# Third stage of a hybrid decoder trunk run in two passes over its tiles, with the next weights split inside them

## The chip, the cores and the metric

The kernel runs on one core of a Trainium2 chip. A core has TensorE for matmuls (PE in the profile, PEld for its weight loads), VectorE (DVE), ScalarE (ACT) and GpSimd (POOL), and SyncE (SP), which here only issues DMAs. The metric is the device time of one execution in microseconds (us), lower is better.

## The reference

The trunk has two layers over 16 meta tokens and 2048 tokens of width 1024, in float32. What the change touches is the end of layer 0, the shared keys and values, and the input and output of layer 1:

```python
        h = h + gated_deltanet_mixer(h, ...)          # ends with  o @ w_out
    kv = rmsnorm(h, kv_norm) @ kv_w + kv_b            # k gets the rotary embedding
    proj = rmsnorm(h, norm_g) @ w_in                  # queries and gate z of layer 1
    q = apply_rope(proj[..., :SWA_Q_W] + b_q)
    o = sink_attention(q, k, v, ...) * jax.nn.silu(z)
    h = h + o @ w_out
    y = rmsnorm(h, final_norm)                        # meta tokens dropped
```

Each matmul with weights is done as three, of a high and a low part of either operand (high x high, high x low, low x high). Weights are split for that into a high part (ACT: a copy that rounds, with the norm's gain as scale) and a low part (DVE: the rest), chunk by chunk, from a staging buffer that a DMA fills.

## The kernel before

Four stages run one after the other, each with its own buffers and semaphores: normalise_and_transpose, gated_deltanet, output_and_shared_kv (the third stage, about 1674 to 2216 us of the trace) and attention (the fourth). Within a stage every engine has its own program, in order, and waits on semaphores.

The third stage works on 17 tiles of 128 tokens, T = 0 the meta tokens. For tile T it loads o (load_o, line 1436), splits it on ACT (split_o, line 1499) and POOL (line 1662), multiplies by w_out (out_projection, line 1684: two halves b of 24 matmuls into ps_h[b]), adds the residual on DVE (add_residual, line 1580, into h1), normalises on ACT (normalise, line 1506), transposes on TensorE (transpose, line 1715), splits the transposed tile into hT (high_part on ACT, low_part on DVE), and multiplies hT by w_kvz (kv_gate, line 1694: 24 matmuls for keys and values, 48 for the gate). DVE and ACT then make keys (keys_values, line 1598) and gate (gate_part, line 1618, with gate_sigmoid on ACT), SP stores h1, hT, v, kT and gate.

The order within the tile loop (tiles, line 1403) is in step: out_projection(T), kv_gate(T - 1), transpose(T) on TensorE (line 1725). So while the chain from the residual of tile T to its hT runs, TensorE has the 72 matmuls of the tile before. SP's step (line 1445) issues the loads of x and o of tile T + 1 first. hT[0] and hT[1], o_s, o_raw and each ps bank are single buffers; h1 and the rotary table cs have two.

Ahead of the loop all weights are split: 8 chunks of w_out (512 KB) and 16 of w_kvz (256 and 512 KB in turn), over three staging buffers (hn, gate and h1's second half, lines 1397 to 1400; loads at line 1480, ACT at 1565, DVE at 1650 and 1652). The meta tile's first product runs along with them, everything after it waits for all 24.

The fourth stage takes hT of 16 tiles from memory. It starts by splitting 8 chunks of w_q (lines 1935, 2040, 2176), with the first query projection following chunk by chunk (line 2286); then 8 chunks of w_out_b between its first two steps (run, line 1842: `between` after step(-1)), and only after them does SP go on to hT of tile 1. Before that SP issues 22 small and middle loads for the keys and values of the meta tokens and of tile 0. step(t) on TensorE (line 2353) mixes the logits and values of tile t with the output projection of tile t - 1 and the query projections of t + 1 and t + 2; its second full one is step(1).

Of the kernel before, what the change touches and what calls it, by code (L numbers as in the profile page):

```python
# [8 lines left out]
P = 128  # L9
# [1318 lines left out]
def output_and_shared_kv(nc, x, meta, w_out, w_kvz, gains, kv_b, rope, consts, oT_d, oTm_d, h1_d, hT_d, gate_d, kT_d, v_d):  # L1328


    with nc.cleanup_on_exit(), ExitStack() as ctx:
# [11 lines left out]
        kv = sb("p3_kv", [P, KVW])  # L1343
        swapped = sb("p3_swapped", [P, KVW // 2])
        kv_bias = sb("p3_kvb", [P, KVW])
        kT = sb("p3_kT", [P, 2, P])
        gate = sb("p3_gate", [P, 2, FB])
        sig = sb("p3_sig", [P, FB])
        cs = sb("p3_cs", [P, 2, 2 * HD])
# [10 lines left out]
        const_in = sem("p3_const_in")  # L1360
        w_in = [sem(f"p3_w_in{n}") for n in range(3)]
        w_hi = sem("p3_w_hi")
# [12 lines left out]
        hT_lo = sem("p3_hT_lo")  # L1375
        kv_ps = sem("p3_kv_ps")
# [9 lines left out]
        hT_out = sem("p3_hT_out")  # L1386
# [5 lines left out]
        N_CONST = 3  # L1392
        block = ctx.enter_context(nc.Block())

        stage = (hn[:], gate[:].rearrange("p b k -> p (b k)"), h1[:, 1, :])
        chunks = [(wo, kc, slice(0, D), w_out, None) for kc in range(KC)]
        for kc in range(KC):
            chunks += [(wk, kc, slice(0, KVW), w_kvz, kc), (wk, kc, slice(KVW, KZ), w_kvz, KC + kc)]  # L1400


        def tiles(eng, step):

            step(0, 0, True, False)
            step(1, 1, True, True)
            step(2, 0, True, True)
            with eng.Fori(1, NT // 2 - 1) as j:
                for s in (1, 0):
                    step(2 * j + (2 - s), s, True, True)  # L1410
            step(NT - 1, 1, True, True)
            step(NT, 0, True, True)
            step(NT + 1, 1, False, True)

        def is_meta(T):
            return isinstance(T, int) and T == 0

        def rows_of(T):
            return META if is_meta(T) else P

        @block.sync
        def _(sp):
            def load_x(T, s):
                if isinstance(T, int) and T == 2:
                    sp.wait_ge(hn_ready, 1)
                elif not (isinstance(T, int) and T < 2):
                    sp.wait_ge(h1_out[s], 16 * ((T - 1) // 2))
# [1094 lines left out]
```

## Time and profile before

| | before |
|---|---|
| median of 3 runs | 2982.18 us (2980.31 to 2986.79) |
| the profiled execution's own time | 2984.5 us |
| its span, first to last instruction | 2982.5 us |
| mean granted TensorE clock | 0.938 |
| busy PE / DVE / ACT / POOL | 86% / 53% / 38% / 20% of the span |
| third stage | about 1674 to 2216 us |
| fourth stage | about 2217 us to the end |

The busy shares are means over stages with different limits, so they are to be read stretch by stretch. The granted clock is the share of full speed that the chip gave TensorE: 1.00 is 2.4 GHz, 0.50 is 1.2 GHz, and a value between is a stretch that had both. In a timeline each row is a run of equal instructions on one engine; in brackets stands how long the engine was idle before it, and what released it. PE, PEld, DVE, ACT and POOL are the engines, SPq is SP's queue of DMA issues.

### The profile page before, as it was taken

Reading aid. Unit: us, or ns where it says so; the run is one execution under the profiler, and the core shown is the slowest. Engines: PE = TensorE matmul, PEld = TensorE weight load, DVE = VectorE, ACT = ScalarE, POOL = GpSimd, SP = SyncE. Lnnn points to the kernel's source line nnn. Section 1 sums busy time; section 2 is a strip of 40 time slices with the busy share of each in tenths; the row PEclk is TensorE's granted clock in tenths of the full one; section 3 lists DMA queues with packets and bytes.
Section 4 is the critical chain, followed back from the end, with each engine's and each line's share of the span. In section 5 each row is a group of like instructions: output and inputs, shape, how many; then the busy total and the mean of one; then the engine's idle time right before and its main releaser. Section 6 shows DMA issues by size and latency. Waiting matters only on the chain. (4 is left out here: it accounts for less than half of the span.)

```text
span 2982.5 us, 51249 instructions
## 1 busy us (share of the span) xinstructions
PE 2575.0 (86%) x17497; PEld 2284.2 (77%) x17497; DVE 1586.5 (53%) x3692; ACT 1122.8 (38%) x3278; POOL 595.6 (20%) x509
## 2 busy tenths in 40 slices
PE   5468888899999999999998569999966999999996
PEld 4367777888888888888887348888855778778875
DVE  4256666676777677777676322222224444444443
ACT  4244454544444444444443323333323232323222
POOL 0043333311111121111111000000002232322321
PEclk8689999999999999999998579999987999999998
DMA  9764354534436443443441334333333121121211
GB/s 249 226 238 149 116 179 138 172 125 138 129 110 208 123 132 122 136 132 114 144 129 45 115 115 138 108 128 130 106 133 129 64 80 57 62 79 64 70 49 45
DMA packets 272982, 367.27 MB, mean 123 GB/s; under 512 B 74626, under 2 KB 191442, under 8 KB 272882
## 3 DMA queue, kind: packets, MB, share of 16 engines
q1 hardware_dynamic: 231762, 340.64, 35.0%
q10 hardware_dynamic: 41120, 25.37, 2.9%
q8 instruction: 54, 0.88, 0.1%
q14 instruction: 46, 0.38, 0.0%
HBM read 246.96 MB, written 118.98 MB: 123 GB/s over the span
## 5 line engine op out<-in xcount | busy, mean ns | idle before, releaser
L1176 PE MATMUL p_psp<-xg,p_whi 128*128 128x264 f32 x4096 | 847.5, 297 | 25.6 <-POOL p_wlo L1107 19.6
L1176 PEld LDWEIGHTS p_psp<-xg,p_whi 128*128 128x128 f32 x4096 | 666.7, 194 | 28.7 <-issue 26.4
L1176 PE MATMUL p_psp<-xg,p_wlo 128*128 128x264 f32 x2048 | 614.6, 300 | 0.0
L1176 PEld LDWEIGHTS p_psp<-xg,p_wlo 128*128 128x128 f32 x2048 | 397.9, 194 | 0.0
L2235 PE MATMUL p_psq<-p_wq,p_hT 128*128 128x512 f32 x768 | 216.0, 419 | 39.2 <-DVE p_wq L2176 28.7
L954 DVE SCALAR_TENSOR_TENSOR p_acc<-p_proj,p_taps,p_acc 128x528 f32<-128x528 f32 x288 | 242.3, 841 | 8.2
L1680 PE MATMUL p_psh<-p_wo,p_o 128*128 128x512 f32 (+1 forms) x816 | 198.4, 403 | 27.1 <-DVE p_wo L1650 23.3
L975 DVE TENSOR_TENSOR p_prod<-p_Xb,p_blk 32x4 f32<-32x4 f32 (+13 forms) x448 | 202.2, 451 | 5.6
L1680 PEld LDWEIGHTS p_psh<-p_wo,p_o 128*128 128x128 f32 (+1 forms) x816 | 149.9, 186 | 69.3 <-issue 20.6
L2235 PEld LDWEIGHTS p_psq<-p_wq,p_hT 128*128 128x128 f32 x768 | 139.9, 195 | 73.9 <-issue 22.6
L2235 PE MATMUL p_pso<-p_wo,p_oT 128*128 128x512 f32 x768 | 189.2, 399 | 5.1 <-DVE p_oT L2130 5.1
L836 ACT ACTIVATE p_sig<-p_sig 128x528 f32<-128x528 f32 x128 | 82.6, 645 | 278.6 <-DVE p_sig L956 278.2
L1680 PE MATMUL p_psz<-p_wk,p_hT 128*128 128x512 f32 x768 | 176.7, 389 | 0.0
L2235 PEld LDWEIGHTS p_pso<-p_wo,p_oT 128*128 128x128 f32 x768 | 142.2, 190 | 37.0 <-DVE p_oT L2130 8.8
L1680 PEld LDWEIGHTS p_psz<-p_wk,p_hT 128*128 128x128 f32 x768 | 144.2, 188 | 29.9
L1107 POOL TENSOR_TENSOR p_wlo<-p_wraw,p_whi 128x512 fp32r<-128x512 f32 x72 | 100.2, 1402 | 257.4 <-ACT p_whi L817 256.8
L1662 POOL TENSOR_TENSOR p_o<-p_oraw,p_o 128x1024 fp32r<-128x1024 f32 (+1 forms) x17 | 38.8, 2281 | 489.4 <-ACT p_o L1504 489.4
L1983 ACT ACTIVATE p_logits<-p_logits,p_top 128x144 f32<-128x144 f32 x256 | 102.6, 402 | 79.9 <-DVE p_top L2091 79.9
L2339 PEld LDWEIGHTS p_psq<-p_v,p_pT 128*128 128x128 f32 x992 | 119.2, 192 | 16.5 <-issue 11.4
L828 ACT ACTIVATE p_proj<-p_psp 128x264 f32<-128x264 f32 x256 | 99.8, 390 | 72.8 <-PE p_psp L1176 70.7
L1999 ACT ACTIVATE p_out<-p_h 128x1024 f32<-128x1024 f32 x16 | 16.9, 1058 | 278.7 <-DVE p_h L2138 278.7
L2339 PE MATMUL p_psq<-p_v,p_pT 128*128 128x64 f32 x992 | 117.5, 271 | 0.0
(265 smaller groups left out, 4746.3 us busy)
## 6 DMA issues: line engine op xcount, KB each, us to landing
p_whi<-w_dram SPq DMA_DIRECT2D x92, 512.0 KB, 4.3
p_wlo<-w_dram SPq DMA_DIRECT2D x92, 512.0 KB, 5.4
p_wraw<-w_a_in SPq DMA_DIRECT2D x36, 512.0 KB, 6.1
w_dram<-p_whi SPq DMA_DIRECT2D x34, 512.0 KB, 4.1
w_dram<-p_wlo SPq DMA_DIRECT2D x34, 512.0 KB, 5.2
xg<-xT_dram SPq DMA_DIRECT2D x8, 2112.0 KB, 13.1
hT_dram<-p_hT SPq DMA_DIRECT2D x32, 512.0 KB, 2.9
p_hT<-hT_dram SPq DMA_DIRECT2D x32, 512.0 KB, 4.3
```

The lines of the kernel that those rows point to most:

```text
L828: nc.scalar.activation(proj[:, f % 2, 3 + half_ * HALF:3 + (half_ + 1) * HALF], ps_p[half_][:, 0:HALF], ACT.Copy).then_inc(proj_read, 1)
L836: ins = nc.scalar.activation(v, v, ACT.Exp, scale=-1.0)
L954: nc.vector.scalar_tensor_tensor(a, p[:, part:part + GW], w, a, ALU.mult, ALU.add).then_inc(tap_done, 1)
L975: link(nc.vector.tensor_tensor(t3, x3[:, 0:i, 0:i].rearrange("p j c -> p c j"), b3[:, 0:i, i].unsqueeze(1).to_broadcast([rows, i, i]), ALU ...
L1107: nc.gpsimd.tensor_tensor(w_lo[:, f, cols], w_raw[:, f % 2, cols], w_hi[:, f, cols].bitcast(f32), ALU.subtract).then_inc(lo_ready, 1)
L1176: ins = nc.tensor.matmul(ps_p[half_][:, 0:HALF], (w_hi, w_lo)[i][:, f, kc * P:(kc + 1) * P], xg[:, g % 2, j, kc, half_ * HALF:(half_ + 1) ...
L1662: nc.gpsimd.tensor_tensor(o_s[1][:, :, 0:rows], o_raw[:, :, 0:rows], o_s[0][:, :, 0:rows].bitcast(f32), ALU.subtract).then_inc(o_lo, 1)
L1680: last = nc.tensor.matmul(out, stationary[i][:, kc, 0:rows], moving(j, kc), start=kc == 0 and n == 0, stop=kc == KC - 1 and n == 2)
L1983: last_ = nc.scalar.activation(logits[:, s_, :], logits[:, s_, :], ACT.Exp, bias=top[:, s_:s_ + 1], accum_out=den[:, s_:s_ + 1])
L1999: link(nc.scalar.activation(out[:], h[:], ACT.Square, accum_out=rinv[:]))
L2235: ins = nc.tensor.matmul(banks[b][:], stationary[i][:, kc, :], weights[j][:, kc, b * FB:(b + 1) * FB], start=kc == 0 and n == 0, stop=kc = ...
L2339: last_ = nc.tensor.matmul(ps_q[b][:, cols], pT[:, g % 2, x, n * P:(n + 1) * P], v[:, slot, kvh * HD:(kvh + 1) * HD], start=False, stop=g ...
```

## The change

The third stage goes over its tiles twice. The first pass does, per tile, the output projection, the residual, the normalising, the transposes and the split of hT, which is stored for all 17 tiles (the meta tile's in a new array hTm). The second loads hT again, two buffers ahead (in the buffers that held o), and does keys, values and gate. Only w_out is split ahead of the first pass. Each tile T = 0 to 15 of the first pass also loads and splits one chunk of w_kvz; each tile T = 1 to 8 of the second one chunk of w_q, into the buffers that w_out had, which now outlive the stage (first_w) and are handed to attention. o is split into two buffers by turns; o_raw, kv, swapped, sig and kT share one buffer (work), and kv_bias and cs lie in h1's second half. All loops of the stage are written out instead of a hardware loop. The product's halves are taken apart: the transposes of the tile before stand between them, and the turning of the keys stands between the two halves of the gate. The fourth stage has no w_q, no gain, and splits w_out_b in two lots of four chunks, after step(-1) and after step(0), over two staging buffers; SP's load of hT of tile 1 comes ahead of the first lot, h1 of tile 0 behind the second.

The diff, cut to its core:

```diff
--- before.py
+++ after.py
-        wo = [sb(f"p3_wo{n}", [P, KC, D], f32r) for n in range(2)]
+        T_ALL = NT + 1
+        wo = wq = first_w
         wk = [sb(f"p3_wk{n}", [P, KC, KZ], f32r) for n in range(2)]
-        o_raw = sb("p3_oraw", [P, KC, P])
-        o_s = [sb(f"p3_o{n}", [P, KC, P], f32r) for n in range(2)]
+        o_s = [[sb(f"p3_o{s}{n}", [P, KC, P], f32r) for n in range(2)] for s in range(2)]
+        hT_in_sb = o_s
...
-        stage = (hn[:], gate[:].rearrange("p b k -> p (b k)"), h1[:, 1, :])
-        chunks = [(wo, kc, slice(0, D), w_out, None) for kc in range(KC)]
-        for kc in range(KC):
-            chunks += [(wk, kc, slice(0, KVW), w_kvz, kc), (wk, kc, slice(KVW, KZ), w_kvz, KC + kc)]
-
-
-        def tiles(eng, step):
-
-            step(0, 0, True, False)
-            step(1, 1, True, True)
-            step(2, 0, True, True)
-            with eng.Fori(1, NT // 2 - 1) as j:
-                for s in (1, 0):
-                    step(2 * j + (2 - s), s, True, True)
-            step(NT - 1, 1, True, True)
-            step(NT, 0, True, True)
-            step(NT + 1, 1, False, True)
-
-        def is_meta(T):
-            return isinstance(T, int) and T == 0
-
-        def rows_of(T):
-            return META if is_meta(T) else P
+        early = (hn[:], gate[:].rearrange("p b k -> p (b k)"), h1[:, 1, :])
+        k_stage = gate[:].rearrange("p b k -> p (b k)")
+        q_stage = hn[:]
...
+        K_CHUNKS = [(kc, cols, g) for kc in range(KC) for cols, g in ((slice(0, KVW), kc), (slice(KVW, KZ), KC + kc))]
+
+        def k_chunk_of(T):
+
+            return T if T < 2 * KC else None
+
+        def q_chunk_of(T):
+            return T - 1 if 1 <= T <= KC else None
...
+            def load_x(T):
+                s = T % 2
+                if T == 1:
+                    sp.wait_ge(w_lo, KC)
+                elif T >= 2:
+                    if T >= 3:
+                        sp.wait_ge(h1_out[s], 16 * ((T - 1) // 2))
+                    sp.wait_ge(hn_ready, T - 1)
...
+            def load_k_chunk(n):
+                sp.wait_ge(w_lo, KC + n)
+                kc, cols, _ = K_CHUNKS[n]
+                sp.dma_start(k_stage[:, 0:cols.stop - cols.start], w_kvz[:, kc, cols]).then_inc(k_in, 16)
+
+            def load_q_chunk(kc):
+                sp.wait_ge(w_lo, 3 * KC + kc)
+                if kc == 0:
+                    sp.wait_ge(hT_ps, T_ALL)
+                    sp.wait_ge(h_ps, 2 * T_ALL)
+                sp.dma_start(q_stage, w_q[:, kc, :]).then_inc(q_in, 16)
...
+            def load_hT(T):
+
+                s = T % 2
+                sp.wait_ge(h_ps, 2 * T_ALL)
+                sp.wait_ge(hT_out, 32 * (T + 1))
+                if T >= 2:
+                    sp.wait_ge(kv_ps, T - 1)
+                if T >= 3:
+                    sp.wait_ge(z_ps, 2 * (T - 2))
+                for part in range(2):
+                    sp.dma_start(hT_in_sb[s][part][:, :, 0:rows_of(T)].bitcast(f32), hT_home(T, part)
+                                 ).then_inc(hT_in[s], 16)
...
+            for T in range(T_ALL + 1):
+                if T + 1 < T_ALL:
                     load_o(T + 1)
-                if new and not is_meta(T):
+                    load_x(T + 1)
+                if k_chunk_of(T) is not None:
+                    load_k_chunk(k_chunk_of(T))
+                if T:
+                    store_hT(T - 1)
+                if 1 <= T < T_ALL:
+                    s = T % 2
                     sp.wait_ge(h_ready, 2 * (T + 1))
-                    sp.dma_start(h1_d[bass.ds(T * P - P, P), :], h1[:, s, :]).then_inc(h1_out[s], 16)
-                if old:
-                    o = T - 1
-                    rows = rows_of(o)
-                    sp.wait_ge(k_turned, o + 1)
-                    sp.dma_start(v_d[o][0:rows, :], kv[0:rows, KVW // 2:]).then_inc(v_out, 16)
-                if not (isinstance(T, int) and T >= NT):
-                    load_table(T + 1, 1 - s)
-                if old:
-                    sp.wait_ge(kT_ready, o + 1)
-                    sp.dma_start(kT_d[o][:, :, 0:rows], kT[:, :, 0:rows]).then_inc(kT_out, 16)
-                if new and not is_meta(T):
-                    for part, ready in ((0, hT_hi), (1, hT_lo)):
-                        sp.wait_ge(ready, 2 * (T + 1))
-                        sp.dma_start(hT_d[T - 1][part], hT[part][:].bitcast(f32)).then_inc(hT_out, 16)
-                if old and not is_meta(T - 1):
+                    sp.dma_start(h1_d[(T - 1) * P:T * P, :], h1[:, s, :]).then_inc(h1_out[s], 16)
+                if T == T_ALL - 1:
+                    load_hT(0)
+                    load_hT(1)
+                    sp.wait_ge(hn_ready, T_ALL - 1)
+                    sp.wait_ge(h1_out[1], 16 * (NT // 2))
+                    sp.dma_start(kv_bias, kv_b.partition_broadcast(P)).then_inc(bias_in, 16)
+                    load_table(0)
...
+            for T in range(T_ALL + 1):
+                if T + 1 < T_ALL:
+                    load_table(T + 1)
+                if T < T_ALL:
+                    if q_chunk_of(T) is not None:
+                        load_q_chunk(q_chunk_of(T))
...
                     sp.wait_ge(gate_ready, 2 * (T - 1))
                     sp.dma_start(gate_d[T - 2], gate[:]).then_inc(gate_out, 16)
-
-            load_o(0)
-            load_x(0, 0)
-            load_table(0, 0)
-            for dst, src in ((ident[:], consts["ident"]), (gain[:], gains), (kv_bias[:], kv_b.partition_broadcast(P))):
-                sp.dma_start(dst, src).then_inc(const_in, 16)
-            for n, (_, kc, cols, src, _) in enumerate(chunks):
-                if n >= 3:
-                    sp.wait_ge(w_lo, n - 2)
-                sp.dma_start(stage[n % 3][:, 0:cols.stop - cols.start], src[:, kc, cols]).then_inc(w_in[n % 3], 16)
-            sp.wait_ge(w_lo, len(chunks))
-            tiles(sp, step)
+                if T < T_ALL:
+                    sp.wait_ge(kT_ready, T + 1)
+                    sp.dma_start(kT_d[T][:, :, 0:rows], kT[:, :, 0:rows]).then_inc(kT_out, 16)
+                if T + 2 < T_ALL:
+                    load_hT(T + 2)
...
+                if T >= 2:
+                    act.wait_ge(h_ps, 2 * (T - 1))
...
+            for T in range(T_ALL + 1):
+                if T + 1 < T_ALL:
+                    split_o(T + 1)
+                if T:
+                    normalise(T - 1)
+                if k_chunk_of(T) is not None:
+                    k_chunk_high(k_chunk_of(T))
+                if T:
+                    high_part(T - 1)
+            for T in range(T_ALL + 1):
+                if T >= 2:
+                    gate_sigmoid(T - 1, 1)
+                if q_chunk_of(T) is not None:
+                    q_chunk_high(q_chunk_of(T))
+                if 1 <= T < T_ALL:
+                    gate_sigmoid(T, 0)
+                if T < T_ALL:
+                    keys_out(T)
...
+            for T in range(T_ALL + 1):
+                if k_chunk_of(T) is not None:
+                    k_chunk_low(k_chunk_of(T))
+                if T < T_ALL:
+                    add_residual(T, 0)
+                if T:
+                    low_part(T - 1)
+                if T < T_ALL:
+                    add_residual(T, 1)
+            for T in range(T_ALL + 1):
+                if T >= 2:
+                    gate_part(T - 1, 1)
+                if q_chunk_of(T) is not None:
+                    q_chunk_low(q_chunk_of(T))
+                if T < T_ALL:
+                    keys_values(T)
+                if 1 <= T < T_ALL:
+                    gate_part(T, 0)
...
+            for T in range(T_ALL + 1):
+                if T < T_ALL:
+                    out_projection(T, 0)
+                if T:
+                    transpose(T - 1)
+                if T < T_ALL:
+                    out_projection(T, 1)
+            for T in range(T_ALL):
+                keys_values(T)
+                if T:
+                    gates(T, 0)
+                turn_keys(T)
+                if T:
+                    gates(T, 1)
...
+            if weights is not None:
+                weights(0, KC // 2)
             step(0, 0, True, True, False)
+            if weights is not None:
+                weights(KC // 2, KC)
             step(1, 1, True, True, True)
...
+                    if n >= 2:
+                        sp.wait_ge(w_lo, n - 1)
+                    sp.dma_start(stage[n % 2], w_out[:, n, :]).then_inc(w_in[n % 2], 16)
+                if end == KC:
+                    load_h1(0)
...
-            load_weights(0, KC)
             load_keys(0, 0)
...
-                    if is_first(t) and b == 0:
-                        pe.wait_ge(w_lo, kc + 1)
...
+    with nc.sbuf_tensor("first_w0", [P, KC, D], f32r) as high, nc.sbuf_tensor("first_w1", [P, KC, D], f32r) as low:
+        output_and_shared_kv(nc, d["x"], d["meta"], d["w_out"], d["w_kvz"], d["w_q"], d["kv_b_gains"], d["kv_b"],
+                             d["rope"], c, [high, low], scratch["oT"], scratch["oTm"], scratch["h1"], scratch["hT"],
+                             scratch["hTm"], scratch["gate"], scratch["kT"], scratch["v"])
+        attention(nc, d["w_out_b"], d["b_q"], d["sinks"], d["final"], d["rope"], c, [high, low], scratch["h1"],
+                  scratch["hT"], scratch["gate"], scratch["kT"], scratch["v"], out)
```

## Rows read from the trace of the kernel before

**Rows 1.** Busy time by stretch; columns in the head row, (x) counts instructions.

```profile
core 0: us, PE busy (x) PEld busy (x) DVE busy (x) ACT busy (x) POOL busy (x), PEclk, DMA share, GB/s
...
1702.00:1740.00 38.00, 9.33 (x35) 3.87 (x35) 18.20 (x21) 18.34 (x24) 2.00 (x1) 0.59 0.62 188
...
1800.00:2160.00 360.00, 360.00 (x1650) 299.43 (x1649) 100.76 (x164) 113.81 (x189) 31.22 (x13) 1.00 0.35 121
```

**Rows 2.** Timeline (start us, us, engine, line, what, count), one steady tile, TensorE.

```profile
1962.63 11.15 PE L1680 MATMUL p_psh<-p_wo,p_o 128*128 128x512 f32 x48
...
1973.62 5.60 PE L1680 MATMUL p_pskv<-p_wk,p_hT 128*128 128x512 f32 x24
...
1990.95 11.15 PE L1680 MATMUL p_psh<-p_wo,p_o 128*128 128x512 f32 x48
```

**Rows 3.** Timeline, same tile: residual sum, normalising, split of o, low part.

```profile
1973.82 0.69 DVE L1586 TENSOR_TENSOR p_h<-p_psh,p_h 128x512 f32<-128x512 f32 x1 [4.69 <-PE p_psh L1680]
...
1974.62 1.06 ACT L1511 ACTIVATE p_hn<-p_h 128x1024 f32<-128x1024 f32 x1 [7.05 <-DVE p_h L1586]
...
1976.37 1.15 ACT L1514 ACTIVATE p_hn<-p_h,p_rinv 128x1024 f32<-128x1024 f32 x1
...
1977.42 1.04 ACT L1504 ACTIVATE p_o<-p_oraw 128x1024 fp32r<-128x1024 f32 x1
...
1992.02 1.29 DVE L1593 TENSOR_TENSOR p_hT<-p_pst,p_hT 128x512 fp32r<-128x512 f32 x2 [3.82 <-ACT p_hT L1525]
```

**Rows 4.** Line 1442, loads of o: time from issue to landing.

```profile
DMA to landing us min/median/max: 3.8/5.3/6.1
```

**Rows 5.** DMA issues, 1674 to 2216 us and all: count, size, median us to landing.

```profile
p_gate<-w_kvz_in SPq DMA_DIRECT2D x2, 512.0 KB, 3.9
...
p_gate<-w_kvz_in SPq DMA_DIRECT2D x3, 256.0 KB, 2.7
...
p_hT<-hT_dram SPq DMA_DIRECT2D x32, 512.0 KB, 4.3
```

**Rows 6.** Splits of w_kvz by line (ns min/median/max), then timeline of the head.

```profile
L1565 ACT ACTIVATE p_wk<-p_h,p_gain x6: 707/934/1152, 1701.4 to 1728.9; 128x512 fp32r<-128x512 f32 x3, 128x1024 fp32r<-128x1024 f32 x3
...
L1652 DVE SCALAR_TENSOR_TENSOR p_wk<-p_h,p_gain,p_wk x6: 742/1016/1285, 1702.7 to 1730.1; 128x512 fp32r<-128x512 f32 x3, 128x1024 fp32r<-128x1024 f32 x3
...
1702.79 8.30 PE L1680 MATMUL p_psh<-p_wo,p_o 128*16 128x512 f32 x27 [3.11 <-DVE p_wo L1650]
...
1740.40 13.10 PE L1680 MATMUL p_psh<-p_wo,p_o 128*128 128x512 f32 x48 [3.83 <-POOL p_o L1662]
```

**Rows 7.** Timeline: keys of a tile on DVE, and matmuls after an idle time.

```profile
1979.42 0.69 DVE L1606 TENSOR_TENSOR p_kv<-p_pskv,p_kvb 128x512 f32<-128x512 f32 x1 [4.91 <-PE p_pskv L1680]
...
1981.79 0.42 DVE L1616 TENSOR_TENSOR p_kv<-p_kv,p_swapped 128x256 f32<-128x256 f32 x1
...
2191.49 7.32 PE L1680 MATMUL p_pskv<-p_wk,p_hT 128*128 128x512 f32 x24 [2.01 <-DVE p_hT L1593]
```

**Rows 8.** Timeline: end of the third stage, start of the fourth.

```profile
2209.54 0.38 PE L1711 MATMUL p_psk<-p_ident,p_kv 128*128 128x128 f32 x2
...
2221.56 0.43 SPq L1934 DMA_DIRECT2D p_sink<-sinks_in  x1
...
2250.85 0.73 POOL L2215 TENSOR_TENSOR p_swapped<-p_q,p_cs 128x256 f32<-128x256 f32 x1 [100.02 <-DVE p_q L2105]
...
2252.65 0.42 SPq L1927 DMA_DIRECT2D p_o<-w_out_b_in  x1
...
2253.71 1.29 POOL L2221 TENSOR_TENSOR p_q<-p_q,p_swapped 128x512 f32<-128x512 f32 x1
...
2276.72 1.76 DVE L2064 MEMSET p_logits<- 128x2048 f32 x1 [0.38 <-issue]
...
2286.11 0.71 PE L2266 MATMUL p_psr<-p_kT,p_qT 64*128 64x128 f32 x8
...
2306.87 1.16 PE L2266 MATMUL p_psr<-p_kT,p_qT 64*128 64x128 f32 x16
```

More of the change, by code:

```diff
@@ new lines, in load_table @@
+            def load_table(T):
+                if T >= 2:
+                    sp.wait_ge(k_turned, T - 1)
+                sp.dma_start(cs[0:rows_of(T), T % 2, :], rope[0:META, :] if T == 0 else
+                             rope[(T - 1) * P + META:T * P + META, :]).then_inc(cs_in[T % 2], 16)
+            load_o(0)
+            load_x(0)
+            for dst, src in ((ident[:], consts["ident"]), (gain[:], gains)):
+                sp.dma_start(dst, src).then_inc(const_in, 16)
+            for n in range(KC):
+                if n >= 3:
+                    sp.wait_ge(w_lo, n - 2)
+                sp.dma_start(early[n % 3], w_out[:, n, :]).then_inc(w_in[n % 3], 16)
@@ L1562, in _ @@
             act.wait_ge(const_in, 16 * N_CONST)
-            for n, (w, kc, cols, _, g) in enumerate(chunks):
+            for n in range(KC):
                 act.wait_ge(w_in[n % 3], 16 * (n // 3 + 1))
-                nc.scalar.activation(w[0][:, kc, cols], stage[n % 3][:, 0:cols.stop - cols.start], ACT.Copy,
-                                     scale=1.0 if g is None else gain[:, g:g + 1]).then_inc(w_hi, 1)
+                nc.scalar.activation(wo[0][:, n, :], early[n % 3], ACT.Copy).then_inc(w_hi, 1)
             act.wait_ge(eps_set, 1)
-            act.wait_ge(w_lo, len(chunks))
-            tiles(act, step)
+            act.wait_ge(w_lo, KC)
+            for T in range(T_ALL + 1):
[8 more added lines that the diff above has]
+            for T in range(T_ALL + 1):
+                if T >= 2:
+                    gate_sigmoid(T - 1, 1)
[5 more added lines that the diff above has]
+                    keys_out(T)
         @block.vector
@@ L1682, in product, with out_projection @@
                 return last
[L1684 removed]
+            def out_projection(T, b):
                 rows = rows_of(T)
[L1686 to L1692 removed]
@@ new lines, in out_projection, with transpose @@
+                if T:
+                    pe.wait_ge(h_ready, 2 * T - (1 - b))
+                product(ps_h[b][0:rows, :], o_s[T % 2], lambda j, kc: wo[j][:, kc, b * FB:(b + 1) * FB], rows,
+                        (lambda kc: pe.wait_ge(w_lo, kc + 1)) if T == 0 and b == 0 else None).then_inc(h_ps, 1)
+            def transpose(T):
+                rows = rows_of(T)
+                pe.wait_ge(hn_ready, T + 1)
+                if T:
+                    pe.wait_ge(hT_lo, 2 * T)
+                for kc in range(KC):
+                    last = nc.tensor.transpose(ps_t[kc // 4][:, kc % 4 * P:kc % 4 * P + rows],
+                                               hn[0:rows, kc * P:(kc + 1) * P], ident[0:rows, 0:rows])
+                last.then_inc(hT_ps, 1)
@@ L1835, in attention, with run @@
         grid = lambda t: t.rearrange("p (c k) -> p c k", k=P)
-        stage = (h[:], out[:], o[:].rearrange("p b k -> p (b k)"))
-        chunks = [(w, kc, src) for w, src in ((wq, w_q), (wo, w_out)) for kc in range(KC)]
-        def run(eng, step, between=None):
+        stage = (out[:], h[:])
+        def run(eng, step, weights=None):
             step(-1, 1, False, True, False)
-            if between is not None:
-                between()
+            if weights is not None:
+                weights(0, KC // 2)
             step(0, 0, True, True, False)
+            if weights is not None:
+                weights(KC // 2, KC)
             step(1, 1, True, True, True)
```

302 lines of the change are left out of this document (119 added, 183 removed).

## The prediction

> **What bounds the kernel now.** I read the busy time by stretch first. In the steady part of the third stage (1800 to 2160 us) TensorE is busy for all 360 us at the full granted clock, 1.00 or 2.4 GHz, and DVE and ACT for less than a third; in the stretch before it, while the stage's weights are still being split, TensorE works 9.3 of 38 us at 0.59 [rows 1]. So the steady part is worth nothing to anybody who doesn't remove matmuls, and what can be won is at the two heads, of this stage and of the next. The timeline of one steady tile comes second: 48 matmuls for the residual stream, 24 for keys and values, 48 for the gate, 10 transposes; one tile begins 28.3 us after the other with no gap [rows 2]. With 1.0 for the transposes that leaves 27.3 / 120 = 0.2275 us a matmul, 10.9 for 48. Third comes what hangs behind a residual sum while TensorE is busy with the 72 other matmuls: normalising takes from 1974.62 to 1977.52, 2.9 us, and splitting the next tile's o another 1.04 [rows 3]. None of that is seen now, because 16.5 us of matmuls lie over it. Last come the transfers: o of a tile lands 3.8 to 6.1 us after its issue, 512 KB of weights in 3.9, 256 KB in 2.7, hT in 4.3 [rows 4, 5].
>
> **What the change removes and moves.** The matmuls stay (1992 in the stage). (a) The first pass needs only w_out, so tile 1 no longer waits for the 16 chunks of w_kvz: now it starts at 1740.40 [rows 6]. (b) The fourth stage no longer splits w_q, and w_out_b is split in two halves inside its first steps. (c) The two passes separate the 48 matmuls of the residual stream from the 72 that covered its chain. (d) One chunk of w_kvz per tile of pass one and one of w_q in tiles 1 to 8 of pass two are loaded and split between the tile's own work. (e) hT is written and read again, 1 MB a tile; h1's stores, the tables and the key and value stores stay.
>
> **Head of the stage.** The last chunk of w_out is split by 1702.8 [rows 6]. Two issues fewer stand in front and no chunk of w_kvz is in flight beside the last one, whose landing took long; I take 1700, between 1697 and 1702.8. The second half of the meta tile's product then takes what it took, 8.3 us [rows 6]: its residual is complete at 1700 + 8.4 + 0.2 + 0.7 = 1709.3. Were nothing else in the way, tile 1 would be 31 us earlier than now.
>
> **Pass one, the step that decides.** Write A for the time at which tile T-1's residual is summed, and follow the queues to the same point of tile T. SP waits for that sum (h_ready) to store h1, and only behind that wait stands, in the next round, load_o(T+1). ACT has split_o(T+1) in front of normalise(T-1). Normalising releases TensorE's transposes, and through hn_ready it releases SP's load_x(T+1), behind which load_k_chunk(T) is issued. DVE has k_chunk_low(T) in front of both add_residual(T). So two transfers lie in series inside each round:
> - store issue and load issue 0.4, o landing 4.5, split 1.04 with its release 0.1, normalising 2.9: A + 9.0 [rows 3, 4]. The landing is bounded by 3.8 (alone) and 5.3 (the median, with x beside it); here an h1 store is beside it, so between them.
> - TensorE's branch: transposes and 24 matmuls 6.3, release 0.3, sum 0.7, and what the idle time before them costs in clock. After 2 us of idleness 24 matmuls took 7.3 instead of 5.6 [rows 2, 7], and after 3.8 us 48 took 13.1 instead of 11.15 [rows 6, 2]; this idleness is about 4 us, so 2. A + 18.2 (16.2 without).
> - DVE's branch: x issue 0.4, chunk landing 3.0 or 4.0 (256 or 512 KB, with x in front; bounds 2.5 to 3.8 and 3.6 to 4.6 around [rows 5]), ACT 0.72 or 1.15, DVE 0.74 or 1.28 [rows 6], the sum 0.69, low parts 1.3, the other sum 0.69 [rows 3]. A + 16.7 for the even chunks, A + 18.6 for the odd.
>
> A round takes the later of the two: 18.2 or 18.6, against 48 matmuls and 8 transposes, 11.7, that TensorE needs. Round 1 lacks the wait for o (loaded under the meta tile's product): 12.9. Round 16 has neither o nor chunk: 11.3. Sum: 1709.3 + 12.9 + 7 x 18.2 + 7 x 18.6 + 11.3 = 1991.1.
>
> A page bears on this. The Trainium skill, "DMA: Bandwidth & Descriptors", Anatomy of one DMA, prices a transfer at about 2.0 us and its bytes at 436 GB/s, an estimate of 3.2 us for 512 KB where the trace has 3.8 and more; by it the rounds would be about 16.9 us and the whole 21 us less than I say. Its Rules for kernel authors ask to issue a DMA early and to wait for it late; that speaks against this order, in which o is asked for when it is next.
>
> **Pass two.** From the last sum: normalising 2.9, transposes 2.0 (twice the 1.0) at the lower clock, the meta tile's 24 matmuls 7.3 [rows 7], keys on DVE 2.8 and 0.2 [rows 7] that nothing covers, since the meta tile has no gate, 0.4 for its turning and 1.5 of clock: 17.1, to 2008.2. hT of tiles 0 and 1, the bias and the table land under that. Then 16 tiles of 72 matmuls and 2 transposes, 16.6 each: 265.6. The next hT is asked for a whole tile ahead and lands in 4.3: hidden. In tiles 1 to 8 the chunk of w_q is issued behind two hT loads and a table, 1.4 us into the tile, lands in 5.5 (3.9 in [rows 5], up to 6.1 in [rows 4], three transfers in flight), is split in 1.15 + 1.28, and only then DVE takes the keys, 2.8: they are ready at 12.2, TensorE wants to turn them at 10.9. 1.3 x 8 = 10.4 (0 to 16). The gates end at 1991.1 + 17.1 + 265.6 + 10.4 = 2284.2, now at 2209.5 [rows 8]: the stage is 74.7 us longer, of which 94.5 come from the rounds over 11.7.
>
> **Fourth stage.** Now TensorE reaches its second full step at 2306.87 [rows 8]. Shifted to the same start: the seven constants, the last issued at about 2221 [rows 8], land at about 2226 (an estimate, as for o); 48 matmuls with the clock's rise (7.3 + 5.5) end at 2239, bias 0.7, rotation of the half (POOL, 4.1 [rows 8]) and transposes at 2246, ACT copies until 2247.2. SP's 22 issues for keys and values, which now hold it until 2252.65 [rows 8], then lie under the projection. Four chunks of w_out_b on two buffers, in two turns of load 3.9, ACT 1.1, DVE 1.3 [rows 5, 6]: DVE is free at 2257.3 and only then sets the logits (now at 2276.72 [rows 8]). TensorE's third group of logits, now at 2286.11 [rows 8], comes at 2260, the next step 20.8 later, at 2281. There the other four chunks stand in front of DVE's second merge, asked for behind hT of tile 2: DVE is free at about 2290.7, TensorE wants the first copies at 2287 and gets them at 2292, a stall of 5 and one of clock. Gain: 2306.9 - 2281 - 6 = 19.9 (15 to 24). The rest of the stage is the same work.
>
> **Sum.** 74.7 - 19.9 = 54.8 on the profiled execution's 2984.5 us (span 2982.5, 2 around it); that execution is 2.3 above the median of 2982.18. Forecast 3037.
>
> **Rivals.**
> - Pass one keeps TensorE busy (the other side). If SP and ACT were ahead of need, so that o and the chunk lay ready, the rounds would be 11.7 us, 14 rounds of 6.7 less, and 2942 is the time. For it: DVE and ACT together are busy only a third of the time [rows 1]. Against it: the order of the queues, which leaves no way round either transfer. The point from which it decides: each us off the round is worth 14, so the change pays when a round is under 18.4 - 54.8/14 = 14.5. Even with each transfer at its lower bound and no loss of clock the rounds are 15.5 and 17.4. 0.09.
> - The clock stays at its lower level through pass one, as it nearly does in the head, where it reads 0.59 [rows 1]. At 1.2 GHz 48 matmuls and 8 transposes take about 21.3 us, the rounds are TensorE's, and 14 x 2.9 = 41 more give 3078. Against it: 13.1 us for 48 after an idle stretch show that it rises within such a burst. 0.09.
> - The losses cancel the gains within 0.2% (6 us, about what a measurement of this kernel can tell from no change): rounds near 14.5. 0.04.
>
> That it doesn't do what it says I don't see: w_q is split before the fourth stage in any case.
>
> **How the numbers follow.** Forecast 0.78. Low end of its range: transfers at their lower bounds and a warm clock, 27 us less; the earliest w_out 3, no stall for w_q 10, the larger gain at the head 4: 2993. High end: o in 5.3 and slow chunks, 15 more, and 11 for the others: 3063; towards the clock's rival 3078. All bounds at once are unlikely at the low end, so 2998 to 3078. Faster 0.09, same 0.04, slower 0.87.
>
> **What would show it.** In the profile after: from one add_residual to the next of the same half 18 us in pass one; TensorE idle in front of L1721's successor, the transposes, for 4 to 5 us per tile, released by ACT's normalising; ACT idle in front of split_o, released by the DMA of o; DVE idle in front of the w_kvz low part. Rounds under 14.5 make me wrong in sign. Pass two should be 16.6 per tile, with 1 to 2 us before the turning of the keys in the first eight; the fourth stage's second step some 20 us earlier after its start.

## The result, and the profile after

The changed kernel takes 3043.29 us (median of 4 runs, 3039.51 to 3051.53), the kernel before beside it 2983.11 (4 runs). The ratio is 1.0214, with a 95% interval of 1.0199 to 1.0229: it is 2.1% slower.

The two profiled executions are set side by side by stage. A stage is measured from its first load to that of the next, the fourth to the end of the span. These are the three rows of the kernel after:

```profile
core 0 of [0], span 3043.1 us
...
1673.87 0.37 SPq L1434 DMA_DIRECT2D p_work<-oTm_dram  x1
...
2291.26 0.81 SPq L1929 DMA_DIRECT2D p_hT<-hT_dram  x2
```

In the kernel before the same two loads stand at 1674.61 and 2216.91. So the third stage went from 542.3 to 617.4 us, 75.1 longer, and the fourth from 765.6 to 751.8, 13.8 shorter. The stages ahead, whose code is the same, take 0.7 less. In sum 60.6, the difference of the spans.

The windows of after say where in the stage the longer time lies (columns as in [rows 1]): pass one, then a steady part of pass two.

```profile
1712.00:1997.00 285.00, 214.94 (x874) 174.29 (x872) 53.96 (x79) 84.42 (x137) 32.88 (x14) 0.87 0.46 158
2150.00:2284.00 134.00, 133.99 (x598) 110.19 (x596) 38.42 (x72) 32.50 (x56) 0.00 (x0) 1.00 0.30 106
```

Pass two is what the steady stage was before [rows 1]: TensorE busy all the time, clock 1.00. In pass one TensorE is idle for 70 of 285 us and the clock reads 0.87. The 16 stores of h1 mark the rounds: the first at 1719.55, the fifteenth at 1985.73, the last at 1996.94. That is 19.0 us for each of rounds 2 to 15, where 48 matmuls and 8 transposes need 11.8.

One even round of pass one, in the timeline of after (start us, us, engine, line, what, count; in brackets the idle time and its releaser). L1542 splits o, L1549 to L1552 normalise, L1744 transposes, L1567 and L1646 split the chunk, L1631 adds the residual:

```profile
1757.39 0.33 SPq L1496 DMA_DIRECT2D h_dram<-p_h  x1
1757.76 0.69 SPq L1438 DMA_DIRECT2D p_work<-oT_dram  x1
1763.10 1.06 ACT L1542 ACTIVATE p_o<-p_work 128x1024 fp32r<-128x1024 f32 x1 [8.49 <-DMA p_work<-oT_dram]
1764.07 1.04 ACT L1549 ACTIVATE p_hn<-p_h 128x1024 f32<-128x1024 f32 x1
...
1765.79 1.15 ACT L1552 ACTIVATE p_hn<-p_h,p_rinv 128x1024 f32<-128x1024 f32 x1
1766.99 1.97 PE L1744 MATMUL p_pst<-p_ident,p_hn 128*128 128x128 f32 x8 [5.58 <-ACT p_hn L1552]
...
1767.40 0.43 SPq L1444 DMA_DIRECT2D p_gate<-w_kvz_in  x1
1768.61 9.71 PE L1725 MATMUL p_psh<-first_w,p_o 128*128 128x512 f32 x36
1771.05 0.72 ACT L1567 ACTIVATE p_wk<-p_gate,p_gain 128x512 fp32r<-128x512 f32 x1 [4.11 <-DMA p_gate<-w_kvz_in]
...
1775.64 0.69 DVE L1631 TENSOR_TENSOR p_h<-p_psh,p_h 128x512 f32<-128x512 f32 x1 [1.29 <-PE p_psh L1725]
1776.37 0.33 SPq L1496 DMA_DIRECT2D h_dram<-p_h  x1
```

The reader is to follow one string through it: the h1 store is issued, behind it o is asked for, o lands, ACT splits it, and only then normalises a tile whose sum had been there for 6.7 us (since 1757.36); that releases both the transposes and, through SP, the chunk. The last sum waits 1.29 us for TensorE. An odd round, with its chunk of 512 KB, ends otherwise:

```profile
1747.61 0.43 SPq L1444 DMA_DIRECT2D p_gate<-w_kvz_in  x1
...
1752.49 1.15 ACT L1567 ACTIVATE p_wk<-p_gate,p_gain 128x1024 fp32r<-128x1024 f32 x1 [5.35 <-DMA p_gate<-w_kvz_in]
1753.68 1.28 DVE L1646 SCALAR_TENSOR_TENSOR p_wk<-p_gate,p_gain,p_wk 128x1024 fp32r<-128x1024 f32 x1 [15.29 <-ACT p_wk L1567]
...
1754.88 0.68 DVE L1631 TENSOR_TENSOR p_h<-p_psh,p_h 128x512 f32<-128x512 f32 x1
...
1756.68 0.68 DVE L1631 TENSOR_TENSOR p_h<-p_psh,p_h 128x512 f32<-128x512 f32 x1
```

Here DVE's low part of the chunk and the two sums with hT's low parts between them follow each other without a gap: the second transfer sets the end. The table of waits of after, 1720 to 1990 us (us in total, times, longest), adds up both transfers and the wait of the transposes:

```profile
ACT p_o L1542 <- DMA p_work<-oT_dram: 121.6, 14, 10.3
...
PE p_pst L1744 <- ACT p_hn L1552: 68.8, 14, 6.6
ACT p_wk L1567 <- DMA p_gate<-w_kvz_in: 63.9, 14, 5.9
```

### The profile page after: what moved, and what is told of

Same layout as the page of the kernel before. It is cut to its first block and busy times, and to the rows that moved or that the text cites. A ratio compares the mean times of both kernels' runs of the same rounds, so it can differ in the third digit from the quotient of the medians.

```text
span 3043.1 us, 50787 instructions
## 1 busy us (share of the span) xinstructions
PE 2602.3 (86%) x17497; PEld 2300.4 (76%) x17497; DVE 1572.2 (52%) x3692; ACT 1118.3 (37%) x3278; POOL 593.4 (19%) x509
## 5 line engine op out<-in xcount | busy, mean ns | idle before, releaser
L1725 PE MATMUL p_psh<-first_w,p_o 128*128 128x512 f32 (+1 forms) x816 | 214.4, 425 | 20.3 <-DVE first_w L1689 19.9
L2274 PE MATMUL p_psq<-first_w,p_hT 128*128 128x512 f32 x768 | 212.1, 414 | 18.5 <-DMA p_sink<-sinks_in 18.0
L1725 PEld LDWEIGHTS p_psh<-first_w,p_o 128*128 128x128 f32 (+1 forms) x816 | 161.4, 201 | 67.5 <-issue 19.5
L1725 PE MATMUL p_psz<-p_wk,p_o 128*128 128x512 f32 x768 | 181.1, 392 | 0.0
L2274 PEld LDWEIGHTS p_psq<-first_w,p_hT 128*128 128x128 f32 x768 | 138.8, 193 | 50.2 <-DMA p_sink<-sinks_in 18.5
L1725 PEld LDWEIGHTS p_psz<-p_wk,p_o 128*128 128x128 f32 x768 | 143.0, 188 | 29.4
L2254 POOL TENSOR_TENSOR p_swapped<-p_q,p_cs 128x256 f32<-128x256 f32 x32 | 23.7, 739 | 554.8 <-DVE p_q L2150 535.9
L2376 PEld LDWEIGHTS p_psq<-p_v,p_pT 128*128 128x128 f32 x992 | 119.2, 192 | 16.6 <-issue 11.7
L1646 DVE SCALAR_TENSOR_TENSOR p_wk<-p_gate,p_gain,p_wk 128x512 fp32r<-128x512 f32 (+1 forms) x16 | 16.3, 1018 | 222.4 <-ACT p_wk L1567 222.4
## 6 DMA issues: line engine op xcount, KB each, us to landing
xg<-xT_dram SPq DMA_DIRECT2D x8, 2112.0 KB, 12.8
```

What stands on the lines that cost most here:

```text
L1725: last = nc.tensor.matmul(out, stationary[i][:, kc, 0:rows], moving(j, kc), start=kc == 0 and n == 0, stop=kc == KC - 1 and n == 2)
L2274: ins = nc.tensor.matmul(banks[b][:], stationary[i][:, kc, :], weights[j][:, kc, b * FB:(b + 1) * FB], start=kc == 0 and n == 0, stop=kc = ...
L2376: last_ = nc.tensor.matmul(ps_q[b][:, cols], pT[:, g % 2, x, n * P:(n + 1) * P], v[:, slot, kvh * HD:(kvh + 1) * HD], start=False, stop=g ...
```

## Experiments

The kernel before ran beside each of them on the same chip, so times are compared by ratios: 1.0214 is the change. Since the first two stages, whose code never changes, begin and end up to 15 us earlier or later from execution to execution (the third began between 1664.94 and 1680.30), each profiled execution is also read by its stages:

| kernel | median us | ratio to before (95%) | third stage us | fourth stage us |
|---|---|---|---|---|
| before | 2983.11 | 1 | 542.3 | 765.6 |
| after | 3043.29 | 1.0214 (1.0199 to 1.0229) | 617.4 | 751.8 |
| k_ahead | 3039.44 | 1.0184 (1.0167 to 1.0201) | 608.8 | 754.7 |
| o_ahead | 2960.79 | 0.9929 (0.9910 to 0.9948) | 531.1 | 752.0 |
| ok_ahead | 2945.82 | 0.9874 (0.9858 to 0.9891) | 520.8 | 752.5 |
| fill_gap | 3051.55 | 1.0244 (1.0214 to 1.0273) | 621.6 | 755.7 |
| fill_idle | 3045.43 | 1.0187 (1.0172 to 1.0201) | 616.2 | 752.6 |
| okq_ahead | 2944.59 | 0.9856 (0.9843 to 0.9868) | 511.5 | 752.4 |
| one_lot | 2943.87 | 0.9862 (0.9824 to 0.9901) | 510.2 | 755.6 |
| head_lots | 2927.31 | 0.9803 (0.9791 to 0.9816) | 509.9 | 741.5 |

The seven versions whose fourth stage is the change's own lie between 751.8 and 755.7 there, so a difference of 4 us in one trace's stage is not read as an effect.

My theory was that two transfers in series make the round: o stands in front of both branches and the chunk only in DVE's, so that moving o gives much and moving the chunk alone little. Its rivals: the clock, lowered by the idle time, makes the rounds; or the transfers share a bandwidth that is used up, and asking earlier brings nothing.

**o_ahead: o is asked for one round earlier.**

```diff
+            load_o(1)
             for T in range(T_ALL + 1):
                 if T + 1 < T_ALL:
-                    load_o(T + 1)
                     load_x(T + 1)
                 if k_chunk_of(T) is not None:
                     load_k_chunk(k_chunk_of(T))
+                if T + 2 < T_ALL:
+                    load_o(T + 2)
                 if T:
                     store_hT(T - 1)
```

> One edit to the changed kernel: SP issues the load of o for tile T+2 in round T, behind the chunk of w_kvz and in front of the store of hT, so one round earlier. Theory of the serial chain (the load of o and the load of the chunk lie one after the other in each round of pass one): a round loses the 0.4 + 5.0 us of issue and landing; what is left is split 1.1, normalising 2.9, issue 0.4, chunk 4.3 or 3.5, its two splits, two sums and the low part: 13.9 for odd rounds and 12.1 for even, against 19.1 and 18.9 now; 14 rounds x 6 us = 84, so about 2959 us, faster than the kernel before. Rival, bandwidth (the extra hT traffic fills the queues and the rounds are as long as their transfers take together): the same bytes move, rounds stay near 19, 3043. Rival, clock: the idle gap before the transposes is what costs; it goes too, but then only 2 us a round, 3015.

Measured: ratio 0.9929; moving one load in SP's queue takes 86 us off the third stage and makes the kernel faster than the one before. The rounds are 11.8 us in the even tiles and 13.7 in the odd ones. The waits in 1720 to 1990:

```profile
ACT p_wk L1569 <- DMA p_gate<-w_kvz_in: 73.9, 14, 7.6
...
ACT p_o L1544 <- DMA p_work<-oT_dram: 1.2, 1, 1.2
```

The wait for o went from 121.6 to 1.2. The chunk is now the last thing in both kinds of round: ACT waits for it in all 14, and DVE's last sum waits for TensorE in one of them alone (waits, 1720 to 1900):

```profile
DVE p_h L1633 <- PE p_psh L1727: 1.2, 1, 1.2
```

With 256 KB this string takes 11.2 to 11.4 us in five of the seven even rounds, about what TensorE needs itself; with 512 KB it is longer, and TensorE waits.

**k_ahead: only the chunk is asked for earlier,** behind the store of hT instead of behind x.

```diff
-                if k_chunk_of(T) is not None:
-                    load_k_chunk(k_chunk_of(T))
+                if T == 0:
+                    load_k_chunk(0)
                 if T:
                     store_hT(T - 1)
+                if k_chunk_of(T + 1) is not None:
+                    load_k_chunk(k_chunk_of(T + 1))
```

> The other edit alone: the load of the w_kvz chunk of tile T+1 is issued in round T, behind the store of hT, instead of behind the load of x in round T+1; o stays late. Theory of the serial chain: TensorE's branch (o landing, split, normalising, then transposes and 24 matmuls at a clock that has to rise again) already takes 18 to 19 us, so taking the chunk out of the chain gives only 0 to 0.7 us a round: 3033 to 3043 us. If instead the two transfers were additive whatever the rest does, 14 x 4.3 = 60 us less, 2983.

Measured: ratio 1.0184, rounds of 18.4 and 18.1. ACT no longer waits for the chunk at all (no such row is left in 1720 to 1990), but it waits longer for o:

```profile
ACT p_o L1544 <- DMA p_work<-oT_dram: 159.1, 14, 13.0
...
PE p_pst L1746 <- ACT p_hn L1554: 59.7, 14, 5.3
```

Taking 63.9 us of waiting away brought 0.8 us a round; TensorE's branch, which hangs on o alone, is nearly as long.

**ok_ahead: both.**

> Both edits together: o two tiles ahead and the chunk one tile ahead. Theory of the serial chain: no transfer is left in a round, what is left is split 1.1, normalising 2.9, then 0.8 + 5.5 + 0.9 on TensorE and DVE, and the rounds are TensorE's 11.7 to 12.5: 14 x 6.5 to 7.3 = 91 to 102 us less than the changed kernel, 2941 to 2952 us. Bandwidth rival: 3 MB a round at the 200 to 250 GB/s seen at most over a stretch take 12 to 15 us, so rounds of 13 to 15: 2960 to 2985.

Measured: ratio 0.9874. Every round is 11.78 us. The window and the end of a round:

```profile
1720.00:1880.00 160.00, 160.00 (x764) 133.79 (x763) 50.03 (x69) 74.89 (x119) 31.25 (x13) 1.00 0.74 256
```

```profile
1755.23 1.04 PE L1748 MATMUL p_pst<-p_ident,p_hn 128*128 128x128 f32 x8
1756.03 7.29 PE L1729 MATMUL p_psh<-first_w,p_o 128*128 128x512 f32 x31
...
1762.48 0.33 SPq L1500 DMA_DIRECT2D h_dram<-p_h  x1
```

TensorE is busy in 160.00 of 160.00 us at clock 1.00 while 256 GB/s are moved, where the changed kernel moved 158. So the bandwidth rival falls. In the third stage k alone gives 8.6 us, o alone 86.3, both 96.6: the two gains nearly add, and the small one is small because TensorE's branch is left standing without it.

**fill_gap: is it the clock?** Ahead of the transposes TensorE does 18 matmuls that nobody reads.

```diff
+                if 1 < T < T_ALL:
+                    for _ in range(18):
+                        nc.tensor.matmul(ps_k[:], o_s[T % 2][0][:, 0, :], wo[0][:, 0, 0:FB], start=True, stop=True)
                 if T:
                     transpose(T - 1)
```

> Added to the changed kernel: 18 matmuls (128x512, into a bank that pass one doesn't use, result unused) on TensorE between the first half of the output projection and the transposes, tiles 2 to 16, 4.1 us at the full clock, in the gap in which TensorE waits for the normalised tile. It measures what the clock costs. Theory of the serial chain: the even rounds, in which TensorE's branch is last, get 1.5 us shorter, the odd ones, in which DVE's branch is last, nothing: 3033 us. If the clock were the main cost, 2 us in each of 15 rounds: 3013. If the clock doesn't matter: 3043 or a little more.

Measured: ratio 1.0244, no gain. That was a miss, and the run was a poor test: behind the 18 matmuls TensorE was again idle for up to 2.7 us, in three rounds the transposes still took 1.8 to 2.0, and in round 16, which has no idle time, they stood on the path (15.2 instead of 11.2 us).

**fill_idle: the same with 26 in the even rounds, 17 in the odd, none in round 16.**

> Changes the kernel after alone: ahead of the eight transposes of pass one TensorE gets matmuls that nobody reads, 26 in front of the even tiles and 17 in front of the odd ones (2 to 15), none in front of tile 16; about as much as it is idle there (6.5 and 4.3 us). The first run of this kind had 18 everywhere, left 2.3 us idle in the even rounds, and its transposes still took 1.97 us. Clock theory (the lower clock after the idle time lengthens the even rounds, which end on TensorE): transposes 1.1 instead of 1.97 and 48 matmuls 11.2 instead of 12.4, so seven rounds shorter by about 1.7, 12 us, and 3031. Rival (both branches are set by the transfers, TensorE's slack swallows what the clock costs): within 4 us of 3043. If I have put in too many, the matmuls are on the path themselves and it gets slower.

Measured: ratio 1.0187 with an interval that overlaps that of the change, third stage 616.2 against 617.4. The window of pass one and an even round:

```profile
1720.00:1990.00 270.00, 245.85 (x1115) 199.22 (x1114) 50.72 (x75) 81.10 (x130) 33.44 (x14) 0.99 0.46 157
```

```profile
1801.06 0.33 SPq L1496 DMA_DIRECT2D h_dram<-p_h  x1
...
1804.93 6.05 PE L1779 MATMUL p_psk<-first_w,p_o 128*128 128x512 f32 x26
...
1810.87 1.09 PE L1744 MATMUL p_pst<-p_ident,p_hn 128*128 128x128 f32 x8
...
1811.72 11.19 PE L1725 MATMUL p_psh<-first_w,p_o 128*128 128x512 f32 x48
...
1818.78 0.33 SPq L1496 DMA_DIRECT2D h_dram<-p_h  x1
```

Now the clock is 0.99 all through, the transposes take 1.09 and the 48 matmuls 11.19; from the transposes to the next store it is 7.7 us on average in the even rounds, 9.4 before. The rounds are hardly shorter: even ones 18.0 (19.1 in after), odd ones 19.8 (18.9). In the even rounds DVE's branch stands right behind TensorE's: in after the last sum waited 1.3 us on average for TensorE, here in five of the seven not at all, so little more than the 1.2 us that they gained was to be had. Two things gave the rest back. In the even rounds 0.45 us went to fillers that ended after ACT and 0.3 to a slower issue. In the odd rounds o took 5.5 us from issue to split instead of 4.8: the stores of hT were issued until 0.4 us ahead of the store of h1, not 1.6, so the load of o had them beside it. Both theories were half right: the clock does lengthen the branch by 1.8 us, as I had priced it, and getting that back is worth little: 1.2 us of the stage in these two traces, 8 us by the ratios (0.0027), whose intervals overlap. That the odd rounds lost because o was asked for into busier queues rests on means of seven rounds in one trace each and isn't tested by itself.

**okq_ahead: in pass two, w_q's chunk too.** ok_ahead, and:

```diff
                 if T < T_ALL:
-                    if q_chunk_of(T) is not None:
-                        load_q_chunk(q_chunk_of(T))
                     rows = rows_of(T)
                     sp.wait_ge(k_turned, T + 1)
                     sp.dma_start(v_d[T][0:rows, :], kv[0:rows, KVW // 2:]).then_inc(v_out, 16)
+                    if q_chunk_of(T + 1) is not None:
+                        load_q_chunk(q_chunk_of(T + 1))
```

> The version with o and the w_kvz chunks issued ahead (2945.8), and in pass two the chunk of w_q issued one tile earlier, behind the store of the values. My account of pass two: the stall ahead of turning the keys (0.2 to 2.2 us in eight tiles, 6.7 in all) is the landing of that chunk, so it goes: 2940. Rival (DVE's own queue is what is late): the stalls stay and so does 2946.

Measured: the row `PE p_psk L1773 <- DVE p_work L1676` of pass two goes from 8.7 us in 8 waits to 2.2 in one, that of the meta tile; the third stage is 511.5 instead of 520.8. So 6.5 us of those waits belonged to the chunks; the meta tile has none, and its 2.2, which the expectation had counted among them, stay. By the ratios the whole kernel gains 0.0018, 5 us, and the intervals overlap. DVE's own queue is not what was late.

**one_lot: what is the halving of w_out_b worth?** okq_ahead, with `weights(0, KC)` ahead of step(0) and nothing behind it.

> As okq_ahead, but all eight chunks of w_out_b are split in one lot ahead of the first step of the fourth stage, as the kernel before had them, and none ahead of the second step. It asks what the halving of this lot is worth within the shorter fourth stage. My account: two more turns of load and split (6.1 us each in okq_ahead's trace) stand in front of DVE's merging in the first step, so TensorE's wait there grows from 5.9 to about 18 us, and the wait of 6.3 in the second step goes: the fourth stage, first load to end, is about 6 us longer than okq_ahead's 752.4, so 758 to 759, and of the 13.8 us that the change wins there about half belong to the halving, the rest to w_q being ready. Rival (TensorE has other work for the wait, or the loads overlap): 752 to 754.

Measured: the fourth stage is 755.6, 3.2 longer, within what the stage varies. The mechanism is there: TensorE's wait in the first step is 17.97 us instead of 5.9, that of the second step is gone.

```profile
2242.24 1.23 PE L2307 MATMUL p_psr<-p_kT,p_qT 64*128 64x128 f32 x8 [17.97 <-DVE p_logits L2123]
```

12.1 more and 6.3 less should be 5.8; but here the constants happened to land 0.7 us sooner and the 48 matmuls behind them took 12.49 instead of 13.73, so 2.0 of it didn't show. By these rows some 3 to 6 of the 13.8 us that the fourth stage won belong to the halving; the times of the whole kernel (0.9862 against 0.9856) don't tell the two apart. How the rest divides between w_q's missing chunks and SP's earlier issues wasn't tried.

**head_lots: both waits of that head.** okq_ahead, with w_out_b in three lots, the first ahead of the results of the first query projection:

```diff
+            if weights is not None:
+                weights(0, 4)
             step(-1, 1, False, True, False)
             if weights is not None:
-                weights(0, KC // 2)
+                weights(4, 6)
             step(0, 0, True, True, False)
             if weights is not None:
-                weights(KC // 2, KC)
+                weights(6, KC)
             step(1, 1, True, True, True)
```

SP loads the first four ahead of load_keys(0, 0), the other four behind step(-1), and h1 of tile 0 behind step(0).

> As okq_ahead, and in the fourth stage w_out_b is split in three lots instead of two: four chunks ahead of the first query projection's results (DVE and ACT have nothing to do there), two ahead of the first step and two ahead of the second, all loaded as soon as their buffer is free. My account of this head: TensorE waits 5.8 us in the first step and 6.4 in the second for logits that DVE merges only after its lot of low parts, and each lot is as long as it is through loads that are asked for late; both waits go: 12 us less than okq_ahead, 2928. Rival (the waits come from the merging itself, or the loads of keys and masks, now issued behind the first lot, become late): within 4 us of okq_ahead or slower.

Measured: ratio 0.9803, the fourth stage 741.5, 10.9 shorter. step(1) begins 63.6 us and step(2) 107.0 us into the stage; in okq_ahead it is 68.2 and 118.9. The logits of step(1) follow each other without the wait of 6.3:

```profile
2247.49 1.16 PE L2318 MATMUL p_psr<-p_kT,p_qT 64*128 64x128 f32 x16
...
2253.16 1.16 PE L2318 MATMUL p_psr<-p_kT,p_qT 64*128 64x128 f32 x16
```

In the first step the wait of 5.9 is gone too; part of it came back ahead of the turning of the first queries, where TensorE waits 7.7 us for POOL instead of 4.9. This is the best version found, 2.0% faster than the kernel before.

## Why the prediction was right

The forecast was 3037 us, the range 2998 to 3078, slower at 0.87; it came to 3043.29. By its own steps:

**Head of the stage.** w_out was split by 1698.4 (I took 1700), the meta tile's sum came at 1707.7 (1709.3); 0.7 of these 1.6 us is the stage's earlier begin. The first store of h1 comes at 1719.55, in the kernel before at 1754.26: the 35 us earlier start is real, and at 7.2 us over TensorE's need it is used up within five rounds.

**Rounds.** 19.0 us against 18.2 and 18.6. The branch that ends a round was named rightly for both kinds, TensorE even, DVE odd. The size was short because of the transfers. Loads of o and of the chunks in after, from issue to landing (min/median/max, the second over both sizes of chunk):

```profile
DMA to landing us min/median/max: 3.6/5.0/7.0
```

```profile
DMA to landing us min/median/max: 3.4/4.1/5.4
```

I had o in 4.5, between [rows 4]'s ends, and the chunks in 3.0 and 4.0; by size they took 3.5 and 4.3. By rounds, o took 5.3 (median) in the even ones, which end on TensorE, and 4.5 in the odd ones: the 0.8 in the even rounds and the chunk's 0.3 in the odd ones are about what the rounds are longer (19.1 against 18.2, 18.9 against 18.6). The profile before had both values: 5.3 is the median of [rows 4], and the view of [rows 5] had a second row of 256 KB chunks,

```profile
p_h<-w_kvz_in SPq DMA_DIRECT2D x3, 256.0 KB, 3.5
```

beside the one of 2.7 that I worked from. The idle time ahead of the transposes was 5.6 us in the round shown where I had worked with 4, so the clock cost 1.8 in an even round, near the 2 I gave it. Round 16 took 11.2 (11.3). From the meta tile's sum to the last it is 289.2 us, 7.4 more than my 281.8.

**Pass two.** Tile 1 began at 2010.6, 13.7 us after the last sum where I had 15.6, and the 1.5 of clock that I had added is there (its first 24 matmuls took 7.16). The tiles without w_q take 16.59 (16.6). The stalls ahead of the turning were 6.7 in eight, but 2.2 of them are the meta tile's, which has no chunk; tiles 2 to 8 have 4.5, and tile 1 none, where I had 10.4 for tiles 1 to 8. The chunk landed in 5.4 (I had 5.5); it was the keys that DVE made in 2.1 us, not 2.8. From the start of tile 1 to the last gate it is 273.4 us, where I had 277.5. So three terms were too high, by 1.6, 1.9 and 4.1, and one too low by 7.4: that the stage came out at +75.1 where I had +74.7 is in part luck. The mis-sized step is the round, by 3%, through the landing times.

**Fourth stage.** I expected 19.9, the trace shows 15.0 at step(2) and 13.8 at the end. The rows of after:

```profile
2302.02 13.62 PE L2274 MATMUL p_psq<-first_w,p_hT 128*128 128x512 f32 x48 [18.03 <-DMA p_sink<-sinks_in]
...
2336.67 1.23 PE L2305 MATMUL p_psr<-p_kT,p_qT 64*128 64x128 f32 x8 [5.83 <-DVE p_logits L2121]
...
2358.85 1.16 PE L2305 MATMUL p_psr<-p_kT,p_qT 64*128 64x128 f32 x16
...
2370.85 2.08 PE L2305 MATMUL p_psr<-p_kT,p_qT 64*128 64x128 f32 x16 [6.25 <-DVE p_logits L2121]
...
2409.55 1.16 PE L2305 MATMUL p_psr<-p_kT,p_qT 64*128 64x128 f32 x16
```

The steps were the right ones; each was a little late. The constants landed 10.8 us into the stage instead of 9.1, the 48 matmuls behind them took 13.6 instead of 12.8: 2.5. From the third group of logits to step(1) 22.2 instead of 20.8: 1.4. The second lot of w_out_b cost 7.4 (50.7 us for the step, 43.3 in the kernel before) instead of 6: 1.4. The whole forecast was short by 6, and this stage alone by 6.1 (13.8 against 19.9), since the third stage's errors cancel.

**The rivals.** "Pass one keeps TensorE busy" at 2942 is what ok_ahead shows, 2945.8, once both transfers are asked for early: its price was right, its condition was not met by the order of the queues. My break-even of 14.5 us a round lies between o_ahead (12.7, faster) and k_ahead (18.2, slower). "The clock stays low" did not happen: 0.87 over pass one. Its price was also too low: at 0.50 the traces have a matmul every 0.43 us and eight transposes in 1.97, so a round is about 22 us, not 21.3.

**The page.** The price that I took from the Trainium skill, "DMA: Bandwidth & Descriptors", Anatomy of one DMA, an estimate of 3.2 us for 512 KB, is given there for transfers that GpSimd issues; SP issues all of these, so no run here tests it, and I shouldn't have carried it over. Of SP's loads only those of x came near it (3.3), chunks of that size took 4.3, o 5.0. Its Rules for kernel authors, to issue early and wait late, is what o_ahead and ok_ahead did, and 97 us of the third stage were the measure of it here.

## What to carry to other kernels

Splitting a loop in two can take away the very work that covered a chain; what then counts is how many transfers the in-order queues put in series in one round, and that is read by following each issue back to the wait that stands in front of it. Take first the transfer on which all branches hang: asking for o one round earlier was worth 86 us, while the chunk, which stands in one branch alone, gave 9. A lowered clock in a starved stretch can be mostly a symptom; here filling the idle time restored the clock, and brought 1 to 8 of the 60 us that the change had cost.

## What the runs showed of the hardware

Most transfers took longer where more was moved, but not all. Rows of the DMA issues between 1720 and 1880 us (count, size, median us to landing), of after, which moved 158 GB/s there, and of ok_ahead, which moved 256:

```profile
hT_dram<-p_hT SPq DMA_DIRECT2D x16, 512.0 KB, 2.6
h_dram<-p_h SPq DMA_DIRECT2D x9, 512.0 KB, 3.7
...
p_gate<-w_kvz_in SPq DMA_DIRECT2D x4, 512.0 KB, 4.3
```

```profile
hT_dram<-p_hT SPq DMA_DIRECT2D x28, 512.0 KB, 3.7
h_dram<-p_h SPq DMA_DIRECT2D x13, 512.0 KB, 2.6
...
p_gate<-w_kvz_in SPq DMA_DIRECT2D x7, 512.0 KB, 5.2
```

A chunk of 512 KB took 0.9 us more, a store of hT 1.1, a load of x 0.3; a store of h1 took 1.1 less and o 0.4 less (4.9 after 5.3). So the mean rate of a stretch doesn't tell a transfer's time; what is in flight beside it may, which wasn't tested. TensorE saw none of it, since every load had most of a round to land in.

The clock after a short pause was not settled by its length. The transposes of pass one, from three traces (after, fill_gap, fill_idle):

```profile
1785.08 1.97 PE L1744 MATMUL p_pst<-p_ident,p_hn 128*128 128x128 f32 x8 [4.04 <-ACT p_hn L1552]
```

```profile
1801.09 1.97 PE L1744 MATMUL p_pst<-p_ident,p_hn 128*128 128x128 f32 x8 [2.28 <-ACT p_hn L1552]
```

```profile
1829.36 1.09 PE L1744 MATMUL p_pst<-p_ident,p_hn 128*128 128x128 f32 x8 [2.60 <-ACT p_hn L1552]
```

The granted clock over these three groups is 0.50, 0.50 and 1.00. In after, with 4.0 us or more of idleness ahead, 12 of the 14 groups took 1.97, the other two 1.4 and 1.8; in the other two all groups behind 2.1 us or less took about 1.1, and between 2.2 and 2.7 both values occur, in three and three. What decides there was left open.
